# Ten of block one's gate tiles made by seven products behind the input norm, with 22 left as filler in the mixers

## The chip, the cores and the metric

The kernel runs on one core of one Trainium2 chip. What is measured is the time of one launch in microseconds (us), the median of three runs. A profiled execution stands beside them; its trace gives start and length of every instruction.

## The reference, cut to what matters

Two transformer blocks over 1024 tokens of width 1024, in fp32. Block one is a layer norm, one wide product, four mixers of width 256 (RET, RWKV, GLA, HGRN), and a gated merge of them:

```
x = layer_norm(x, ln_in_w, ln_in_b)
z = x @ w_in                                 # 1024 x 7696
z_ret, z_rwkv, z_gla, z_hgrn, z_gate = split_cols(z, ...)
branches = (retnet(z_ret), rwkv7(z_rwkv), gla(z_gla), hgrn2(z_hgrn))
for n in range(4):
    merged += sigmoid(z_gate[:, n*1024:(n+1)*1024]) * (branches[n] @ w_branch[n])
```

Behind it come a mixing product, a second norm, a feed-forward part and block two, which the change leaves alone. The change is about z_gate: 4096 columns, 32 tiles of 128.

## The kernel before, in words

**Products.** x lies on the chip transposed (features on partitions) as two parts, x_hi and x_lo, and each fp32 product is made as three: hi by hi, lo by hi, hi by lo. A *strip* is 128 columns of a weight matrix: eight blocks of 128 rows, three products, two halves of 512 tokens, so 48 matmuls of 128x512. Its weights come by a DMA on SP into w_raw, ACT copies them to w_hi (L2084), POOL makes w_lo = w_raw - w_hi (L2103). Two places hold such strips, so that weights run two half-strips or strips ahead of TensorE (class Stream, from L1949). L2152 is the matmul of a plain strip.

**The stages.** `phases` (L5806) calls in turn: `first_group` (0 to 121 us), the RWKV mixer (to 496), HGRN (to 681), GLA (to 871), RET (to some 990), `middle_group` and `second_group`. `first_group` (L3691) makes the input norm (class FirstNorm, L3477: L3680 is its last DVE step) and 16 half strips, (h, j) for h in 0..1 and j in 0..7, the columns of RWKV. ACT mixes each with its neighbour token (L3752), DVE adds the shifted part (L3744, L3746). POOL splits the strips in a loop at the end of the function; each engine's program is one list, done in order.

**The filler.** The mixers' own steps are short matmuls with chains of DVE, ACT and POOL between them. So that TensorE isn't idle there, class Filler (L209) gives it *runs* of six matmuls of 128x512 (L291) of other work: the z columns that the next mixer needs, transposes of its values (a *turn*, two runs a tile, at L284, some 0.6 us a run), and the 32 gate tiles, which go to DRAM and are read back by `middle_group`. A strip is eight runs. Ahead of each step of a mixer class Ring lays as many runs as a table says:

```
def start(self, pe, name, unit):
    self.fill.chunks(pe, self.table.get((name, unit), 0), self.place[name, unit])
    back = self.place[name, unit] - self.pairs
    if back >= 0:
        pe.wait_ge(self.sig["out_" + self.steps[back][0]], self.steps[back][1] + 1)
```

The tables stand by hand in `phases`, a number for each step's name: each mixer has four units n = 0 to 3. Runs left over go at the mixer's end (`rest`, L301). A half strip that is done is copied by ACT from PSUM (L335), which then makes the next w_hi; POOL makes its w_lo before the next thing in its own list (L339 to L347). So where the runs end decides which work of ACT and POOL stands ahead of a mixer's own.

**The steps that the text speaks of.** RWKV: `norm` (ACT L1390, TensorE L1250), `tr1` (DVE L1509, TensorE L1256), X8, TW32, TW64, TA and U (small products with a wait each), `c0` (DVE L1589, TensorE L1328). HGRN and GLA: levels `l0` to `l7` (POOL L1031, L1033 and L1037, TensorE L658), `kt` (TensorE L671, transposes of keys), `psi` (L676, the product for the state; DVE L967 then makes the new state), `y` (L685). RET: `score` (L662), `kt`, `psi`, `y`, `var`, `mean`; its copy before psi is DVE L949.

**The seven products.** In `middle_group` pairs of gate tiles of block two are made by Winograd's form of Strassen's scheme: the product of 256 columns by 1024 tokens is cut in two by two by two, and seven products of 4 row blocks x 3 = 12 matmuls (84 in all) do what 96 do by strips. It needs four sums of x (the forms t1 to t4, class GateForms, L3273: DVE L3293 and L3300, ACT L3315 for their hi part), four sums of weight blocks per pair, and adds of the results. Class GateSevens (L3327) does products (L3404) and adds; class Feed (L2551) brings weights as *units* of 128x512 in six slots and five places: ACT L2659 makes hi, POOL L2686 makes lo, L2663 makes sums of weights.

## Time and profile before

| what | us |
| --- | --- |
| median of three runs | 3285.53 (3285.08 to 3286.27) |
| the profiled execution | 3288.68 |
| its span | 3286.5 |
| TensorE busy | 3244.4 (99%) |
| DVE / ACT / POOL busy | 1872.9 / 1347.6 / 1352.3 |

The span is the time from the first to the last instruction in the trace; some 2.2 us lie around it. TensorE's mean granted clock was 0.997 of its full speed. A row of a timeline reads: start, length, engine, line, operation, result <- operands, sizes, count, and in brackets how long the engine was idle before it and what released it.

### The profile page before, as it was taken

What the parts mean: (1) busy time and instruction counts of PE and PEld (TensorE: products, weight loads), DVE (VectorE), ACT (ScalarE), POOL (GpSimd) and SP (SyncE); (2) the same over time, 40 slices, a digit from 0 to 9 for tenths busy, and PEclk for the clock granted to TensorE, in tenths of its full rate; (3) what the DMA queues carried; (4) which work ended last, traced back from release to release, by engine and by line L of the source; (5) the groups of instructions that cost most, each with busy time, mean ns of one, the idle gap of its engine ahead of it and who ended that gap; (6) DMA issues with size and microseconds to landing.
All of it is one profiled execution on the core that took longest, in us unless ns stands there. A gap on an engine that the chain in (4) does not pass through costs nothing.

```text
span 3286.5 us, 48647 instructions
## 1 busy us (share of the span) xinstructions
PE 3244.4 (99%) x19042; PEld 2622.2 (80%) x19042; DVE 1872.9 (57%) x2504; ACT 1347.6 (41%) x2153; POOL 1352.3 (41%) x850
## 2 busy tenths in 40 slices
PE   9999999999999999999999999999999999999998
PEld 7877787777778878888788878888886888888886
DVE  6333425646446779777783446434663266555678
ACT  5333324343224464333443355224423353445444
POOL 4312124545322846544525654541112665454102
PEclk9999999999999999999999999999999999999999
DMA  4221213232537323333563344332343332345664
GB/s 129 75 65 59 69 56 114 79 100 72 147 93 247 114 80 101 97 106 100 200 200 100 94 120 123 103 117 87 114 133 108 121 96 80 120 157 196 217 194 148
DMA packets 413346, 388.83 MB, mean 118 GB/s; under 512 B 23584, under 2 KB 329632, under 8 KB 410304
## 3 DMA queue, kind: packets, MB, share of 16 engines
q1 hardware_dynamic: 386208, 341.68, 33.8%
q10 hardware_dynamic: 26912, 44.05, 3.9%
q8 instruction: 153, 2.51, 0.3%
q14 instruction: 73, 0.60, 0.1%
HBM read 295.58 MB, written 90.08 MB: 117 GB/s over the span
## 4 chain that ended last, share of the span: by engine, by line
PE 45%; DVE 3%; ACT 1%; issue 1%; POOL 0%; DMA 0%; DVEq 0%; ACTq 0%
PE psum L2152 18%; PE psum L5169 9%; PE psum L2792 8%; PE psum L3404 5%; PE psum L1737 2%; PE psum L1780 1%; PE psum L2828 1%; DVE ffn_form_lo L5158 0%; PE psum L1767 0%; DVE conv L3167 0%; DVE acc L5205 0%; ACT w_hi L2084 0%; PE psum L1755 0%; PE psum L1757 0%; DVE w_lo L2686 0%
## 5 line engine op out<-in xcount | busy, mean ns | idle before, releaser
L2103 POOL TENSOR_TENSOR w_lo<-w_raw,w_hi 128x1024 fp32r<-128x1024 f32 (+1 forms) x226 | 548.1, 2425 | 964.0 <-ACT w_hi L2084 962.0
L2084 ACT ACTIVATE w_hi<-w_raw 128x1024 fp32r<-128x1024 f32 (+1 forms) x227 | 234.6, 1034 | 396.2 <-PE psum L2152 338.9
L291 PE MATMUL psum<-x_hi,w_hi 128*128 128x512 f32 x832 | 355.0, 427 | 3.1 <-ACT gate L335 3.0
L291 PE MATMUL psum<-x_hi,w_lo 128*128 128x512 f32 x832 | 326.9, 393 | 0.0
L291 PE MATMUL psum<-x_lo,w_hi 128*128 128x512 f32 x832 | 326.4, 392 | 0.0
L2152 PE MATMUL psum<-x_hi,w_hi 128*128 128x512 f32 x816 | 312.6, 396 | 3.7 <-DVE w_lo L2112 1.9
L2152 PE MATMUL psum<-x_lo,w_hi 128*128 128x512 f32 x816 | 308.0, 390 | 0.0
L2152 PE MATMUL psum<-x_hi,w_lo 128*128 128x512 f32 x816 | 307.9, 390 | 0.0
L2686 POOL TENSOR_TENSOR w_lo<-w_raw,w_hi 128x512 fp32r<-128x512 f32 x117 | 159.0, 1360 | 127.5 <-ACT w_hi L2659 117.3
L291 PEld LDWEIGHTS psum<-x_hi,w_hi 128*128 128x128 f32 x832 | 156.8, 188 | 48.8 <-issue 14.9
L2152 PEld LDWEIGHTS psum<-x_hi,w_hi 128*128 128x128 f32 x816 | 153.2, 188 | 39.9 <-issue 5.1
L291 PEld LDWEIGHTS psum<-x_hi,w_lo 128*128 128x128 f32 x832 | 156.7, 188 | 35.0
L291 PEld LDWEIGHTS psum<-x_lo,w_hi 128*128 128x128 f32 x832 | 157.2, 189 | 31.9 <-issue 5.8
L2152 PEld LDWEIGHTS psum<-x_lo,w_hi 128*128 128x128 f32 x816 | 153.5, 188 | 33.7 <-issue 2.2
L2152 PEld LDWEIGHTS psum<-x_hi,w_lo 128*128 128x128 f32 x816 | 153.6, 188 | 32.1
L335 ACT ACTIVATE gate<-psum 128x512 f32<-128x512 f32 x115 | 68.1, 592 | 222.3 <-PE psum L291 216.2
L2792 PE MATMUL psum<-x_hi,w_lo 128*128 128x512 f32 x368 | 143.2, 389 | 0.0
L2792 PE MATMUL psum<-x_lo,w_hi 128*128 128x512 f32 x368 | 143.2, 389 | 0.0
L2792 PE MATMUL psum<-x_hi,w_hi 128*128 128x512 f32 x368 | 143.2, 389 | 0.0
L2659 ACT ACTIVATE w_hi<-w_raw 128x512 fp32r<-128x512 f32 x144 | 88.9, 627 | 104.1 <-PE psum L5169 31.3
L5169 PE MATMUL psum<-mlp_form_hi,w_hi 128*128 128x512 f32 x288 | 112.1, 389 | 0.1
L5169 PE MATMUL psum<-mlp_form_hi,w_lo 128*128 128x512 f32 x288 | 112.0, 389 | 0.0
(849 smaller groups left out, 7997.2 us busy)
## 6 DMA issues: line engine op xcount, KB each, us to landing
w_raw<-in_w_in SPq DMA_DIRECT2D x99, 512.0 KB, 4.5
merge_raw<-gates ACTq DMA_DIRECT2D x48, 512.0 KB, 4.7
x_raw<-mlp_forms SPq DMA_DIRECT2D x76, 256.0 KB, 3.4
gates<-gate SPq DMA_DIRECT2D x32, 512.0 KB, 3.0
w_raw<-in_w_mlp_out SPq DMA_DIRECT2D x54, 256.0 KB, 3.3
mlp_forms<-mlp_staged SPq DMA_DIRECT2D x13, 1024.0 KB, 3.9
w_raw<-in_w_ffn_up SPq DMA_DIRECT2D x24, 512.0 KB, 3.9
ffn_x_raw<-ffn_forms SPq DMA_DIRECT2D x46, 256.0 KB, 3.7
```

Source lines behind the costliest of these rows:

```text
L291: last = pe.matmul(bank, w[:, k, :], x[:, k, half(h)], start=(k == 0 and j == 0), stop=(k == KT - 1 and j == 2))
L335: act.activation(self.c.gate[:, n % 2, half(h)], self.c.ps[:, 6 + h, :], ACT.Copy).then_inc(self.sig["g_taken"], 1)
L1737: last = pe.matmul(c.ps[:, 7, :], w[:, k, :], x[:, k, half(h)], start=(k == 0 and j == 0), stop=(k == 7 and j == 2))
L1780: last = pe.matmul(self.o_bank(n)[:, i, :], self.pt[:, n % 2, 2 * i + b, :], self.vs[g][:, j - 1 + b, 64 * h:64 * h + 64], start=(b == hav ...
L2084: act.activation(self.view(self.c.wh, i), self.view(self.c.wr, i), ACT.Copy).then_inc(self.sig["w_hi"], 1)
L2103: pool.tensor_tensor(self.view(self.c.wl, i), self.view(self.c.wr, i), self.view(self.c.wh, i).bitcast(F32), ALU.subtract).then_inc(self.s ...
L2152: last = pe.matmul(self.bank(t, h)[0:m, :], w[:, k, col:col + m], x(k)[:, 512 * h:512 * h + 512], start=(k == 0 and n == 0), stop=(k == nk ...
L2659: act.activation(self.places[self.place_of(u)][0], self.raw(u), ACT.Copy).then_inc(self.sig["f_hi"], 1)
L2686: pool.tensor_tensor(lo, self.raw(u), hi.bitcast(F32), ALU.subtract).then_inc(self.sig["f_pool"], 1)
L2792: last = pe.matmul(self.in_bank(p, n), w[:, k, :], v(k), start=(k == 0 and i == 0), stop=(k == KT // 2 - 1 and i == 2))
L3404: last = pe.matmul(self.bank(p, n), w[:, k, :], v(k), start=(k == 0 and i == 0), stop=(k == KT // 2 - 1 and i == 2))
L5169: ins = pe.matmul(self.bank(i, m), w[:, 0, P * m:P * m + P], x, start=(first and n == 0), stop=(last and n == 2))
```

## The change

Gate tiles 22 to 31 leave the mixers. `first_group` makes them as five pairs by GateSevens, after its 15th half strip and before the 16th. The forms come from a new class FirstForms: DVE first puts x together from its two parts (six quarters of that are POOL's), then makes four sums; ACT copies four hi parts, DVE makes three lo parts and POOL one. The first unit's split with its sums, `feed.lo(pool, 0)`, stands in POOL's loop at half strip 8, units 1 and 2 at 13, units 3 and 4 ahead of the last one. Semaphores are used again under new names. The mixers' gate tiles go from 12, 5, 6 and 9 to 8, 4, 4 and 6, and the tables lose 80 runs: 32 in RWKV, 9 in HGRN, 15 in GLA, 24 in RET. The last argument of each mixer (12 for 15, and so on) says where SP waits for stores.

```diff
     def at(self, name, n):
-        return self.core.counted.get(name, 0) + n
+        return self.here.get(name, self.core.counted.get(name, 0)) + n
+
+    def renew(self, name, old, count):
+
+        self.made[name], self.here[name] = self[old], count
...
@@ -2716,11 +2720,11 @@
 class Freed:
 
 
-    def __init__(self, st, sig, n, done=None):
-        self.st, self.sig, self.n, self.tile = st, sig, n, done
+    def __init__(self, st, sig, n, done=None, own=2):
+        self.st, self.sig, self.n, self.tile, self.own = st, sig, n, done, own
 
     def slot(self, sp, r):
-        if r >= 2:
+        if r >= self.own:
...
+class FirstForms:
...
+    MADE, SPLIT = ("t1", "t3", "t2", "t4"), ("t2", "t3", "t4")
+    READ = {"t1": 4, "t3": 3, "t2": 5, "t4": 5}
...
+    def whole(self, eng, h, k, end):
+        eng.wait_ge(self.sig["x_lo"], KT * h + end)
+        return eng.tensor_tensor(self.x_in[:, k:end, half(h)], self.c.xh[:, k:end, half(h)].bitcast(F32),
+                                 self.c.xl[:, k:end, half(h)].bitcast(F32), ALU.add)
+
+    def whole_pool(self, pool, h, k):
+        self.whole(pool, h, k, k + 2).then_inc(self.sig["x_whole"], 1)
...
+    def sum(self, dve, i):
+
+        x11, x12, x22, x21 = (self.raw[n] for n in self.MADE)
+        if i == 0:
+            self.whole(dve, 1, KT // 2, KT).then_inc(self.sig["gate_t"], 1)
+            return
+        out, x, y = ((x11, x12, x11), (x12, x22, x12), (x22, x22, x11), (x21, x21, x22))[i - 1]
+        dve.wait_ge(self.sig["x_whole"], self.sig.at("x_whole", 6))
+        dve.wait_ge(self.sig["gate_t"], self.sig.at("gate_t", i))
+        dve.tensor_tensor(out, x, y, ALU.subtract).then_inc(self.sig["gate_t"], 1)
+
+    def hi(self, act, name):
+        act.wait_ge(self.sig["gate_t"], self.sig.at("gate_t", self.MADE.index(name) + 2))
+        act.activation(self.his[name], self.raw[name], ACT.Copy).then_inc(self.sig["gate_t_hi"], 1)
...
+    def lo(self, dve, name):
+        self.low(dve, name, 0, 4).then_inc(self.sig["gate_t_lo"], 1)
+
+    def lo_pool(self, pool, k):
+        self.low(pool, "t1", k, k + 2).then_inc(self.sig["gate_t1_lo"], 1)
...
-            self.st.freed_held(pe, self.number(p, n) // 2, hold=1)
+            self.st.freed_held(pe, self.number(p, n) // 2, hold=self.hold)
...
+        def gates_by_sevens(n):
+            flat_place = lambda buf, i: [flat(buf[:, st.place(i)])[:, 512 * b:512 * b + 512] for b in range(2)]
+            slots = [*(more_raw[:, i, :] for i in range(4)), *flat_place(core.wr, n - 1)]
+            places = [(more_w[:, 0, :], more_w[:, 1, :]), *zip(flat_place(core.wh, n - 2), flat_place(core.wl, n - 2)),
+                      *zip(flat_place(core.wh, n - 1), flat_place(core.wl, n - 1))]
+            feed = Feed(sig, slots, places, w_sums, Freed(st, sig, n, own=4))
+            forms = FirstForms(core, sig, raw, low, t_his)
+            def quarter(k0, h):
+                return (lambda k: core.xh[:, k0 + k, half(h)]), (lambda k: core.xl[:, k0 + k, half(h)])
+            x = {"b11": quarter(0, 0), "b21": quarter(4, 0), "b22": quarter(4, 1), **{t: forms.x(t) for t in FirstForms.MADE}}
+            sevens = GateSevens(core, st, sig, feed, forms, x, sum(p is not None for p in st.places), 0)
+            for i in range(gate_tiles[0], gate_tiles[1], 2):
+                sevens.plan(a["w_in"], GATE0 + i * P, gates, (i - KT) * P)
+            feed.elsewhere.update(range(1, sevens.count))
+            st.feeds.append(feed)
+            return feed, sevens, forms
...
+        HELD = 2 * KT - 1
+        for n, (h, j) in enumerate(strips):
+            if n == HELD:
+                st.hold()
+                feed, sevens, forms = gates_by_sevens(st.held)
...
+            st.load(sp, 6)
+            feed.fetch(sp, 3)
+            st.load_held(sp)
+            feed.fetch(sp, len(feed.loads) - 1)
             st.load(sp, len(st.strips))
...
+                if n == HELD:
+                    for p in range(sevens.count):
+                        sevens.tensor(pe, p)
+                if n >= HELD:
+                    sevens.left(pe, n - HELD)
...
-            mixes(2 * KT - 8)
+            mixes(2)
+            forms.hi(act, "t1")
+            feed.hi(act, 0)
+            mixes(1)
+            forms.hi(act, "t3")
+            forms.hi(act, "t2")
+            mixes(1)
+            forms.hi(act, "t4")
+            mixes(2)
+            for u in (1, 2):
+                feed.hi(act, u)
+            mixes(1)
+            for u in (3, 4):
+                feed.hi(act, u)
+            def resume(act, n):
+                if n in (4, 6):
+                    at = st.held + (n - 4) // 2
+                    st.hi(act, st.ends[at - 2], at + 1, True)
+            for p in range(sevens.count):
+                sevens.scalar(act, p, (lambda n: resume(act, n)) if p == sevens.count - 1 else None)
+            sevens.store(act, sevens.count - 1, "c12")
+            mixes(1)
+            sevens.all_stored(act)
...
-            shifts(2 * KT - 8)
+            forms.sum(dve, 0)
+            for i in range(1, 5):
+                forms.sum(dve, i)
+                shifts(1)
+            for name in FirstForms.SPLIT:
+                forms.lo(dve, name)
+                shifts(1)
+            for p in range(sevens.count):
+                sevens.vector(dve, p)
+            shifts(1)
...
+            for n, (h, j) in enumerate(strips):
+                if n == HELD:
+                    for u in (3, 4):
+                        feed.lo(pool, u)
+                    for p in range(sevens.count):
+                        sevens.gpsimd(pool, p)
+                    for i in range(2):
+                        at = st.held + i
+                        st.lo(pool, st.ends[at - 2], at + 1, True)
                 st.lo(pool, tiles[h, j][0])
+                if 2 <= n < 8:
+                    forms.whole_pool(pool, *((0, 0), (0, 2), (0, 4), (0, 6), (1, 0), (1, 2))[n - 2])
+                if n == KT:
+                    feed.lo(pool, 0)
+                if n in (KT + 3, KT + 4):
+                    forms.lo_pool(pool, 2 * (n - KT - 3))
+                if n == KT + 5:
+                    for u in (1, 2):
+                        feed.lo(pool, u)
...
-    slot = first_group(nc, core, a, k, z, col_strip(w, HGRN0, 0), col_strip(w, HGRN0 + 512, 0))
+    slot = first_group(nc, core, a, k, z, gates, (22, 32), col_strip(w, HGRN0, 0), col_strip(w, HGRN0 + 512, 0))
-        gate_tiles(fill, range(12))
+        gate_tiles(fill, range(6, 14))
-        gate_tiles(fill, range(12, 17))
+        gate_tiles(fill, range(14, 18))
-        gate_tiles(fill, range(17, 23))
+        gate_tiles(fill, range(18, 22))
-        gate_tiles(fill, range(23, 32))
+        gate_tiles(fill, range(6))
-                            dict(norm=3, tr1=8, tr2=1, J2=1, J4=1, J8t=1, X4=1, X8=2, TW16=1, Y16=1, TW32=2, Y32=1, TW64=2,
-                                 Y64=1, TA=2, TAt=1, PP=1, c0=2, c1=1, c2=1, c3=1, U=1, y=1, bg=1),
-                            for_hgrn, (col(GLA0 + 512),), (col(GLA0),), [(zt[:, n, :], rows(z_hgrn, n)) for n in (2, 0, 4)], 15)
+                            dict(norm=2, tr1=7, tr2=1, J2=1, J4=1, J8t=1, X4=1, X8=1, TW16=1, Y16=1, TW32=1, Y32=1, TW64=1,
+                                 Y64=1, TA=1, TAt=1, PP=1, c0=1, c1=1, c2=1, c3=1, y=1, bg=1),
+                            for_hgrn, (col(GLA0 + 512),), (col(GLA0),), [(zt[:, n, :], rows(z_hgrn, n)) for n in (2, 0, 4)], 12)
-                              lambda n: dict(var=1, l0=12 if n == 0 else 5, l1=1, l2=1, l3=1, l4=1, l5=1, l6=1, l7=1, kt=3,
-                                             psi=2, y=3 if n == 0 else 2) | (dict(l0=3, kt=4, psi=3) if n == 2 else {}),
+                              lambda n: dict(var=1, l0=10 if n == 0 else 4, l1=1, l2=1, l3=1, l4=1, l5=1, l6=1, l7=1, kt=2,
+                                             psi=2, y=3 if n == 0 else 2) | (dict(l0=3, kt=3) if n == 2 else {}),
-                               *between_rows(zt[:, 0:5:4, :], k["zero"])], 11)
+                               *between_rows(zt[:, 0:5:4, :], k["zero"])], 10)
-                              lambda n: dict(var=1, l0=9 if n == 0 else 5, l1=1, l2=1, l3=1, l4=1,
-                                             l5=1, l6=1, l7=1, kt=2 if n == 0 else 3, psi=2, y=3)
-                              | (dict(l0=3, kt=4, psi=3) if n == 1 else {}),
-                              for_ret, (col(GATE0 + 23 * P),), (col(GATE0 + 24 * P),),
+                              lambda n: dict(var=1, l0=7 if n == 0 else 3, l1=1, l2=1, l3=1, l4=1,
+                                             l5=1, l6=1, l7=1, kt=2, psi=2, y=2),
+                              for_ret, (col(GATE0),), (col(GATE0 + P),),
-                               *between_rows(zt[:, 1:6:4, :], k["zero"])], 11)
+                               *between_rows(zt[:, 1:6:4, :], k["zero"])], 9)
-                              lambda n: dict(score=3 if n == 0 else 2, kt=4, psi=2, y=2, var=3, mean=2), no_mixer,
-                              *((col_strip(a["w_branch"][1], c, 0, rows=2 * P, width=512), 2, P, 512) for c in (0, 512)), [], (0, 1, 3, 5, 9))
+                              lambda n: dict(score=2 if n == 0 else 1, kt=2, psi=1, y=2, var=2, mean=1), no_mixer,
+                              *((col_strip(a["w_branch"][1], c, 0, rows=2 * P, width=512), 2, P, 512) for c in (0, 512)), [], (0, 1, 2, 3, 6))

```

## Rows read from the trace of the kernel before

**Rows 1.** The page: busy time of each engine.

```profile
PE 3244.4 (99%) x19042; PEld 2622.2 (80%) x19042; DVE 1872.9 (57%) x2504; ACT 1347.6 (41%) x2153; POOL 1352.3 (41%) x850
```

**Rows 2.** Waits of TensorE, 125 to 1000 us: total, times, longest.

```profile
PE psum L658 <- POOLq L1037: 5.5, 14, 0.6
```

**Rows 3.** The chain that ended last, around 2060 to 2220 us: start, length.

```profile
2059.99 5.45 PE psum L2152 x24
...
2068.51 149.91 PE psum L3404 x660
```

**Rows 4.** Groups of instructions by line and form: busy time, mean ns of one.

```profile
L3315 ACT ACTIVATE gate_t_hi<-acc 128x2048 fp32r<-128x2048 f32 x4 | 7.6, 1905 | 0.0
...
L2659 ACT ACTIVATE w_hi<-w_raw 128x512 fp32r<-128x512 f32 x144 | 88.9, 627 | 104.1 <-PE psum L5169 31.3 <-DVE w_raw L5114 24.7 <-PE psum L3404 23.8
...
L2686 POOL TENSOR_TENSOR w_lo<-w_raw,w_hi 128x512 fp32r<-128x512 f32 x117 | 159.0, 1360 | 127.5 <-ACT w_hi L2659 117.3 <-DVE ffn_w_raw_more L2663 2.5 <-DVE w_raw L2663 2.5
```

**Rows 5.** Single lines' instructions: ns least, median, most; first and last start.

```profile
L2663 POOL TENSOR_TENSOR ffn_sum<-ffn_w_raw_more,w_raw x1: 1295/1295/1295, 1280.8 to 1280.8; 128x512 f32<-128x512 f32 x1
...
L3300 DVE TENSOR_TENSOR acc<-acc x4: 4307/4370/4376, 2028.7 to 2046.4; 128x2048 f32<-128x2048 f32 x4
```

**Rows 6.** Timeline of ACT and POOL, 86 to 92 us.

```profile
86.47 1.05 ACT L2084 ACTIVATE w_hi<-w_raw 128x1024 fp32r<-128x1024 f32 x1
91.32 0.69 ACT L3752 ACTIVATE rwkv_z<-psum,first_one_mu 128x512 f32<-128x512 f32 x1 [3.80 <-PE psum L2152]
...
87.59 2.39 POOL L2103 TENSOR_TENSOR w_lo<-w_raw,w_hi 128x1024 fp32r<-128x1024 f32 x1 [3.05 <-ACT w_hi L2084]
```

**Rows 7.** Windows: busy by engine (instructions), then granted clock, DMA share, GB/s.

```profile
24.00:27.00 3.00, 3.00 (x10) 2.19 (x9) 2.96 (x5) 1.37 (x2) 2.86 (x3) 0.62 0.06 16
27.00:30.00 3.00, 3.00 (x12) 2.46 (x11) 2.86 (x5) 1.09 (x2) 2.71 (x3) 0.81 0.00 0
```

**Rows 8.** Timeline of RWKV's steps c0, norm (second unit) and tr1.

```profile
197.75 0.69 DVE L1589 TENSOR_TENSOR rwkv_j2t<-rwkv_j2t,rwkv_m_t 128x512 f32<-128x512 f32 x1
198.94 0.38 PE L1328 MATMUL psum<-rwkv_state,rwkv_j2t 128*128 128x128 f32 x2
...
218.39 0.61 ACT L1390 ACTIVATE rwkv_l<-rwkv_jt 128x512 f32<-128x512 f32 x1
...
220.25 1.02 PE L1250 MATMUL psum<-rwkv_l,rwkv_heads 128*128 128x512 f32 x2
...
142.61 0.68 DVE L1509 TENSOR_TENSOR rwkv_j2t<-rwkv_j,rwkv_e_mid 128x512 f32<-128x512 f32 x1
...
143.84 0.60 PE L1256 MATMUL psum<-rwkv_ident,rwkv_j2t 128*128 128x128 f32 x4
```

**Rows 9.** Timeline of GLA: levels of TensorE, and POOL in the first unit.

```profile
785.17 0.68 PE L658 MATMUL psum<-gla_qe,gla_ke 64*64 64x64 f32 x16
...
798.90 0.69 PE L658 MATMUL psum<-gla_qe,gla_ke 64*64 64x64 f32 x32 [0.39 <-POOLq L1037]
...
706.70 2.38 POOL L2103 TENSOR_TENSOR w_lo<-w_raw,w_hi 128x1024 fp32r<-128x1024 f32 x1 [0.17 <-POOL gla_ke L1033]
```

**Rows 10.** Timeline of HGRN's first state update and of y behind it.

```profile
548.87 3.49 DVE L967 SCALAR_TENSOR_TENSOR hgrn_state<-hgrn_state,hgrn_end,hgrn_state_new 128x128 f32<-128x128 f32 x4
...
552.46 0.45 PE L685 MATMUL psum<-hgrn_qe,hgrn_state 128*64 128x128 f32 x4 [0.47 <-issue]
```

**Rows 11.** Timeline of RET's chain from score to psi.

```profile
938.51 1.16 PE L662 MATMUL psum<-mixer_z 64*128 64x128 f32 x16
...
945.94 0.68 DVE L949 COPY ret_k_tok<-psum 128x512 f32<-128x512 f32 x1
...
948.78 1.05 PE L676 MATMUL psum<-ret_v,ret_k_tok 128*128 128x128 f32 x8
```

**Rows 12.** Timeline of RET's first unit: score and the filler behind it.

```profile
882.14 1.16 PE L662 MATMUL psum<-mixer_z 64*128 64x128 f32 x16 [0.58 <-DVE mixer_z L866]
...
889.55 0.47 PE L291 MATMUL psum<-x_hi,w_hi 128*128 128x512 f32 x1 [1.94 <-ACT gate L335]
```

More of the change, by code:

```diff
@@ L123, in __init__ @@
         super().__init__()
-        self.core, self.phase, self.made = core, phase, {}
+        self.core, self.phase, self.made, self.here = core, phase, {}, {}
     def __getitem__(self, name):
@@ L3336, with __init__ @@
     OUT = ("c11", "c22", "c21", "c12")
-    def __init__(self, core, st, sig, feed, forms, x, place):
-        self.c, self.st, self.sig, self.feed, self.forms, self.x, self.place = core, st, sig, feed, forms, x, place
+    def __init__(self, core, st, sig, feed, forms, x, place, hold):
+        self.c, self.st, self.sig, self.feed, self.forms, self.x, self.place, self.hold = (
+            core, st, sig, feed, forms, x, place, hold)
         self.s1, self.u2, self.u3, self.c22 = (core.gate[:, i // 2, half(i % 2)] for i in range(4))
@@ L3699, in first_group @@
     eps, warm = mem("eps", [P, 1]), mem("warm", [P, 1])
+    more_w, more_raw = mem("w_more", [P, 2, T // 2], F32R), mem("w_raw_more", [P, 4, T // 2])
+    w_sums = [at_(f"first_w_sum{i}", [P, T // 2], F32, offset=OFF_TAIL + 2 * KB * i)[:, :] for i in range(2)]
+    low = at_("x_in_lo", [P, KT, T], F32R, offset=OFF_S)
+    t_his = {n: at_(f"first_{n}_hi", [P, KT // 2, T // 2], F32R, offset=OFF_S + (32 + 8 * i) * KB)[:, :, :]
+             for i, n in enumerate(FirstForms.MADE)}
     with ExitStack() as ctx:
@@ L3702, in first_group @@
         st = Stream(core, sig)
+        for i in range(6):
+            sig.renew(f"f_raw{i}", f"x1{i}", 16)
+        for i, name in enumerate(("gate_c11_stored", "gate_c12_stored", "gate_c21_stored", "gate_c22_stored",
+                                  "gate_t_hi", "gate_t_lo", "gate_t1_lo", "gate_s1")):
+            sig.renew(name, f"x0{i}", 16)
+        for name, old, count in (("gate_t", "off", KT), ("gate_sum", "x16", 16), ("f_hi", "x17", 16),
+                                 ("f_pool", "sq_added", KT - 1), ("f_mm", "sq", 2 * KT), ("x_whole", "pair_first", 1),
+                                 ("mixed", "sq_pair", 1), ("carry", "pair", 2), ("carried", "pair_late", 1),
+                                 ("centred", "sq_pair_late", 3), ("log", "shift", 1)):
+            sig.renew(name, old, count)
+        def gates_by_sevens(n):
[14 more added lines that the diff above has]
+            return feed, sevens, forms
         norm = FirstNorm(core, st, sig, raw, sq, total, ones[:, :], eps, w, b, rstd, warm)
@@ L3707, in first_group @@
         norm.plan_var(0)
-        for h, j in strips:
+        HELD = 2 * KT - 1
[3 more added lines that the diff above has]
+                feed, sevens, forms = gates_by_sevens(st.held)
             i = st.strip(col_strip(a["w_in"], RWKV0 + j * P, 0))
@@ L3771, in _ @@
             norm.tensor_sums(pe)
-            for h, j in strips:
+            for n, (h, j) in enumerate(strips):
                 t, i = tiles[h, j]
+                if n == HELD:
[3 more added lines that the diff above has]
+                    sevens.left(pe, n - HELD)
                 if (h, j) == (0, 0):
@@ L4028, in middle_group @@
         in_x = {"b11": quarter(0, 0), "b21": quarter(4, 0), "b22": quarter(4, 1), **{t: forms.x(t) for t in GateForms.MADE}}
-        sevens = GateSevens(core, st, sig, feed2, forms, in_x, sum(p is not None for p in st.places))
+        sevens = GateSevens(core, st, sig, feed2, forms, in_x, sum(p is not None for p in st.places), 1)
         for g in range(3):
```

26 lines of the change are left out of this document (20 added, 6 removed).

## The prediction, made before the changed kernel ran

> **What bounds the kernel now.** I read the busy times first: TensorE is busy 3244.4 of 3286.5 us [rows 1], and no other engine is above 57%. So the time is TensorE's work plus the few places where it waits; the change can only take work away or move waits. Next the waits of the mixer stretch, 125 to 1000 us: the longest entry is 5.5 us in 14 pieces, at L658, released by POOL [rows 2]. The mixers' steps wait little, because a run of filler (six matmuls) or more lies between any two of them. Last, the timeline around single steps: how long ahead of TensorE's step its releaser was done. That slack, held against the time of the run that is taken out in front of the step, is what decides here.
>
> **The work.** Ten strips of 48 matmuls leave the mixers (480, in 80 runs); five pairs of 84 come in (420). A half strip of 24 takes 5.45 us, 0.2271 each and 1.36 a run; the seven products' nearest row is 660 matmuls in 149.91 us, again 0.2271 each, without a wait inside [rows 3]. So -480 + 420 = -60, times 0.2271: **-13.6 us**. The units' transfers and stores go out by SP and ACT in that stretch; the cover is the same as in the row, DMA queues and copies beside 20 us of products a pair, so I cost them at nothing; a late unit would be a wait at L3404. Bounds: -13.6 (as there) to -9 (each pair's first unit late by one ACT copy of 0.63 [rows 4], and 1.5 us for the turn from strips to units).
>
> **The input norm.** ACT mixes strip 9 and makes w_hi of strip 11 until 86.47 + 1.05 = 87.52 us, POOL splits strip 11 from 87.59 on, in 2.39, and TensorE ends strip 10 at 91.3, where ACT's mix of it begins [rows 6]. The change puts on ACT, ahead of that mix, the copy of the form t1 (1.91) and the first unit's copy (0.63) [rows 4]: done at 90.05. On POOL comes, after the split of strip 10 and ahead of that of strip 11, this unit's split of 1.36 [rows 4] and three sums of 1.30 [rows 5], some 0.14 between them: 90.05 to 95.85. POOL's queue is in order, so the split of strip 11 ends at 98.25, and TensorE wants it at 91.3: **7.0** us. I take the order in the code over "it will be ready in time"; had the sums been made before, it would be 3.9 less. What a wait does to the clock: after TensorE's wait of 2 us at 21 to 23 us the granted clock was 0.62 over three us and 0.81 over three more [rows 7]; 3 x 0.38 + 3 x 0.19 = **1.7** us. Together 8.7; bounds 0 (slack in the split that I don't see) and 10.
>
> DVE's form sums are like those of L3300, 4.31 to 4.38 us each in all four places, though POOL's splits run in that stretch [rows 5]; a sum that stood behind a split would be longer. The Trainium skill ("SBUF — State Buffer", section "Who interferes with whom") states that a DVE instruction with two inputs in SBUF and a GpSimd instruction that reads SBUF lock each other out for the whole instruction; by that rule the first form sum would end about 1 us later, and the sum of this forecast would be 1 us higher. In this case the row decides, and it shows no such stretch.
>
> **RWKV, 32 runs fewer, 8 in each of four units.** At X8, TW32, TW64, TA and U the releaser is done over 2 us ahead: these cost nothing; what covers them is that slack and, but for U, the run that stays. Three steps have less slack than a run. c0: DVE's L1589 ends at 198.44, TensorE's L1328 starts at 198.94 [rows 8]: 0.50 against 1.36, so 0.86 lost, four times, 3.4. The norm's step: ACT's L1390 ends at 219.00, L1250 starts at 220.25 [rows 8]: 1.25, 0.1 lost, twice; at the first unit the slack is half of that, 0.8 lost; at the third both runs left are turns of the value tiles, half a run each, 1.8 lost: 2.8. tr1 of the first unit: L1509 ends at 143.29, L1256 starts at 143.84 [rows 8], 0.8 lost. **+7.0**; bounds 0 (DVE's chain starts from a TensorE step that comes earlier by as much) and 10.
>
> **HGRN and GLA, 24 fewer.** (a) Levels 1 to 6 take 785.17 to 798.90, 13.7 us, and end on a wait for POOL [rows 9]: they are paced at 2.3 us a level by POOL and DVE. The shorter l0 moves three to four turns into them, half a run each in place of a whole one, which a level can't give back: 2.7. (b) l0 of GLA's first unit, two runs less ahead of levels whose first products stand on POOL behind a split of 2.38 at 706.70 [rows 9]: all of it lost, 2.7. (c) HGRN's first kt: a strip now ends in the level before, and its split stands ahead of the step's own product on POOL: half a strip's split and copy, 1.6. (d) The state update: DVE's four L967 took 3.49, a POOL split of 2.39 beside them, and L685 waited 0.47 at 552.46 with three runs between [rows 10]. With two runs the same meeting costs 1.36 more, some 1.9. By the counts of runs, splits meet the update at GLA's first and HGRN's last unit (3.0 together) and two old meetings go (-0.9): 2.1. **+9.1**; bounds 2 (only b, in part) and 12.
>
> **RET, 24 fewer.** The chain behind a unit's scores: L662 at 938.51, DVE's masks, a reciprocal, two products, and the copy L949, ending 945.94 + 0.68 = 946.62; L676 follows at 948.78 [rows 11]. The steps are 10.27 apart, 8.1 of them the chain: 2.1 may go, while three runs leave (4.1). So 2.0 is lost at units 1 to 3: 6.0. The first unit's score already waited 0.58, so its run is a wait of 1.4 more; behind it the filler's bank waited 1.94 for ACT [rows 12], and with fewer runs the bank is asked for later, of which 1.2 goes. Its state update meets a split: 1.9. **+8.1**; bounds 2 and 10.
>
> **Sum.** -13.6 + 8.7 + 7.0 + 9.1 + 8.1 = **+19.3 us**. The profiled execution took 3288.68 us (its span 3286.5, and 2.2 around it), 3.15 above the median of 3285.53; its like would be 3308.0, and the median 3304.8. What a measurement can tell from no change is about 0.2%, 6.6 us.
>
> **Rivals.** *Faster* (0.17): ready times move ahead with TensorE. Each mixer chain starts from a TensorE step; if what I took for a fixed chain of DVE starts behind the very step that comes earlier, only its last piece counts, and if POOL's sums fall into its gaps no wait for strip 11 comes. Then -13.6 to -10, 3271.9 to 3275.5. For it: TensorE is busy 99% [rows 1], and the mixers' waits are few [rows 2], so they have been covered amply. Against it: slacks of 0.50 at c0 [rows 8] and 2.1 in RET [rows 11] are smaller than what goes. It decides where slacks exceed 1.36 a run taken out. *Same* (0.12): the mixers absorb it and only the wait for strip 11 comes: -13.6 + 8.7 = -4.9, 3280.6. *Slower still* (0.09), the change not doing what it says: the products of the first stretch stall where those of the middle don't, because strips, forms and units share POOL; one late split of 1.36 [rows 4] in each of five pairs on top of the forecast, 3311.6. It decides once POOL is over a unit behind at the first pair.
>
> **How the numbers follow.** Forecast 0.62, its own range 3292 to 3312: mixer terms at half and at their upper bounds. With the rivals: faster 0.17, same 0.13 (0.12 and a part of the forecast's low end), slower 0.70. The range, 3280 to 3313, takes in the case with the norm's wait alone; it leaves out the one in which all is hidden, and a little above.
>
> **What would show it.** In the changed kernel: 420 matmuls of L3404 in some 95.4 us, starting near 125; at 91 us a wait of TensorE at L2152 for POOL's w_lo, 7 us, and a granted clock under 0.9 in the 6 us behind it; new waits at L1328 (0.9, four), L1250 (0.1 to 1.8), L658 (5.5 to some 10), and L676 of RET (2.0, three). If strip 11 is split ahead of POOL's sums, the norm's term is wrong; if the stretch from the end of the first group to the middle one is shorter by 109 us and not by 85, the mixers' terms are.

## The result and the profile after

The changed kernel takes **3332.0 us** (median of four runs, 3331.8 to 3333.1) against 3285.9 for the kernel before in the same runs: 1.0138 times as long, 95% interval 1.0126 to 1.0151, so 46.1 us slower. The direction was forecast, the size (+19.3) was not, and the time lies above the range. One execution each of experiments 5 and 8 and of the kernel before took 4.6 to 9.0 ms, and the medians and ratios below leave it out, where experiment 8's expectation has it in (3322.4 for 3321.3).

Lines carry new numbers in the changed kernel: the products of the sevens L3404 are L3466, L2152 is L2156, L2103 L2107, L658 L662, L662 (RET's scores) L666, L671 L675, L676 L680, L685 L689, L1328 L1332, L1250 L1254, L1256 L1260, the filler L291 is L295; ACT's copy of a unit L2659 is now L2663, POOL's split of it L2690, its sums L2667, and DVE's form sums are L3363.

First the page after, busy time of each engine, against [rows 1]:

```profile
span 3331.1 us, 48775 instructions
...
PE 3247.0 (97%) x18982; PEld 2618.6 (79%) x18982; DVE 1942.7 (58%) x2563; ACT 1357.9 (41%) x2167; POOL 1412.7 (42%) x887
```

There are 60 matmuls fewer, and yet TensorE is 2.6 us *longer* busy: a matmul takes longer while the clock is low. Where the rest went is in TensorE's waits of the first 1050 us of the changed kernel (line, releaser: us in total, times, longest):

```profile
PE psum L662 <- POOLq L1041: 11.8, 17, 1.9
PE psum L2156 <- POOL w_lo L2107: 11.7, 2, 10.9
PE psum L680 <- DVE ret_k_tok L953: 7.0, 3, 2.4
PE psum L295 <- ACT gate L339: 3.9, 5, 1.4
PE psum L689 <- issue: 3.7, 2, 1.8
PE psum L1332 <- DVE rwkv_j2t L1593: 3.3, 4, 0.8
PE psum L666 <- DVE mixer_z L870: 2.7, 1, 2.7
PE psum L1254 <- ACT rwkv_l L1394: 2.7, 2, 2.0
```

The first is [rows 2] doubled. The second is new, one wait of 10.9 us in the first group. The third and the fifth to the eighth are the steps that the prediction named (psi of RET, y behind the state update, c0, RET's first score, the norm's step).

A table by stage, worked out from TensorE's instructions: a stage runs from its first step to the next one's, the last one to the end of the last matmul, "work" is the change in the number of 128x512 matmuls times 0.2271 us, "lost" is the change of the duration less the work. "Waits" sums idle times over 0.15 us, "clock" sums (1 - granted clock) x busy time over windows of 3 us; both are changes against before.

| stage | before | after | work | lost | waits | clock |
| --- | --- | --- | --- | --- | --- | --- |
| start to first RWKV step | 126.8 | 235.9 | +95.4 | 13.8 | 11.7 | 1.2 |
| to HGRN's first kt | 416.9 | 384.5 | -47.7 | 15.3 | 9.7 | 1.4 |
| to GLA's first kt | 182.4 | 181.2 | -9.5 | 8.3 | 7.4 | 2.4 |
| to RET's first kt | 164.9 | 148.6 | -23.2 | 6.8 | 4.7 | 3.4 |
| to the middle group | 106.4 | 89.5 | -28.6 | 11.7 | 6.8 | 4.5 |
| to the last matmul | 2278.5 | 2280.9 | 0 | 2.4 | 1.7 | 0 |

So 58.3 us lost against 13.6 saved, 44.6 in the spans (46.1 in the medians): some 42 us of it are waits, some 13 the clock, 3 neither column accounts for. Part of these 3 is how idle time is counted: a 128x512 matmul is recorded with 0.39 us though the next starts 0.23 behind it, and a wait counts as idle only from the recorded end. c0 shows it: its four waits are 0.82, and the step comes 0.97 to 0.99 us later than its work says. Over the 19 waits that the mixers have more than before, 0.16 each makes 3 us, by this estimate. The 2.4 of the last row come back in every kernel below (1.7 to 4.2); 1.7 of the 2.4 are waits that I have not followed.

**The long wait.** Timeline of ACT, DVE and POOL in the changed kernel around it (start, length, engine, line):

```profile
86.11 1.92 ACT L3367 ACTIVATE first_t_hi<-x_in 128x2048 fp32r<-128x2048 f32 x1 [0.47 <-DVE x_in L3363]
87.93 0.61 ACT L2663 ACTIVATE first_w_more<-first_w_raw_more 128x512 fp32r<-128x512 f32 x1
...
81.77 4.30 DVE L3363 TENSOR_TENSOR x_in<-x_in 128x2048 f32<-128x2048 f32 x1
...
86.73 2.28 DVE L3363 TENSOR_TENSOR x_in<-x_in 128x2048 f32<-128x2048 f32 x1
...
90.74 2.99 DVE L3363 TENSOR_TENSOR x_in<-x_in 128x2048 f32<-128x2048 f32 x1
...
95.45 2.90 DVE L3363 TENSOR_TENSOR x_in<-x_in 128x2048 f32<-128x2048 f32 x1
...
88.62 1.52 POOL L2690 TENSOR_TENSOR first_w_more<-first_w_raw_more,first_w_more 128x512 fp32r<-128x512 f32 x1 [4.69 <-ACT first_w_more L2663]
90.31 1.27 POOL L2667 TENSOR_TENSOR first_w_sum<-first_w_raw_more 128x512 f32<-128x512 f32 x1 [0.17 <-POOL first_w_more L2690]
91.66 3.20 POOL L2667 TENSOR_TENSOR first_w_sum<-first_w_sum,first_w_raw_more 128x512 f32<-128x512 f32 x1
94.94 1.27 POOL L2667 TENSOR_TENSOR first_w_raw_more<-first_w_raw_more 128x512 f32<-128x512 f32 x1
96.16 6.72 POOL L2107 TENSOR_TENSOR w_lo<-w_raw,w_hi 128x1024 fp32r<-128x1024 f32 x2
```

The queue is as forecast: POOL stands 4.69 us for ACT's copy of the unit with the split of strip 11 behind it, then makes the unit's split and three sums, then the two splits. But one sum takes 3.20 instead of 1.27, and the first of the two splits took 4.4 instead of 2.4 (6.72 for both); each began within 1 us behind a DVE form sum. (Both ends of the wait lie some 1.5 us earlier than in the prediction: TensorE asks at 89.8, ACT's copy of the unit is done at 88.5.)

**The clock.** Windows of the changed kernel (busy of PE, PEld, DVE, ACT, POOL with instructions, then the granted clock, DMA share, GB/s):

```profile
90.00:100.00 10.00, 0.00 (x0) 0.00 (x0) 8.36 (x6) 5.14 (x4) 9.68 (x5) 0.62 0.00 0
100.00:103.00 3.00, 2.30 (x6) 1.85 (x7) 0.00 (x0) 0.00 (x0) 2.88 (x2) 0.50 0.37 99
103.00:106.00 3.00, 3.00 (x9) 2.32 (x8) 0.00 (x0) 0.00 (x0) 0.00 (x0) 0.50 0.90 252
...
974.00:977.00 3.00, 3.00 (x12) 2.65 (x12) 1.34 (x4) 0.00 (x0) 0.70 (x1) 0.58 0.57 176
```

TensorE comes back at 100.7 and works at half speed, 1.2 of 2.4 GHz, for about 5 us. The last row is RET, behind a wait of 2.4 us. The clock's share is the least steady number of this table. Experiments 1, 2 and 5 have the same mixers, with psi waits of 2.39, 2.32 and 2.32 us in each, and their clock column over the four mixer rows sums to 7.4, 7.6 and 9.9, for 11.7 here. In experiment 1 the first two of these waits have no dip behind them; the first, in its timeline and its window:

```profile
967.05 1.13 PE L680 MATMUL psum<-ret_v,ret_k_tok 128*128 128x128 f32 x8 [2.39 <-DVE ret_k_tok L953]
967.00:970.00 3.00, 2.95 (x17) 2.64 (x18) 1.61 (x5) 0.45 (x1) 1.26 (x1) 1.00 0.81 223
```

There RET's stage takes 86.7 us for 89.5. Three single waits of the mixers, in the timeline of the changed kernel:

```profile
302.86 0.46 PE L1332 MATMUL psum<-rwkv_state,rwkv_j2t 128*128 128x128 f32 x2 [0.82 <-DVE rwkv_j2t L1593]
...
744.89 0.45 PE L689 MATMUL psum<-hgrn_qe,hgrn_state 128*64 128x128 f32 x4 [1.83 <-issue]
...
973.43 2.05 PE L680 MATMUL psum<-ret_v,ret_k_tok 128*128 128x128 f32 x8 [2.39 <-DVE ret_k_tok L953]
```

c0 waits 0.82 (forecast 0.86), the met state update 1.83 (1.9), RET's psi 2.39, then 2.32 and 2.31 (2.0).

### The profile page after: what moved, and what is told of

Its sections match the earlier page's. It is cut to its first block and busy times, and to the rows that moved or that the text cites. A ratio compares the mean times of both kernels' runs of the same rounds, so it can differ in the third digit from the quotient of the medians.

```text
span 3331.1 us, 48775 instructions
## 1 busy us (share of the span) xinstructions
PE 3247.0 (97%) x18982; PEld 2618.6 (79%) x18982; DVE 1942.7 (58%) x2563; ACT 1357.9 (41%) x2167; POOL 1412.7 (42%) x887
## 3 DMA queue, kind: packets, MB, share of 16 engines
q1 hardware_dynamic: 384928, 336.44, 32.9%
## 5 line engine op out<-in xcount | busy, mean ns | idle before, releaser
L2107 POOL TENSOR_TENSOR w_lo<-w_raw,w_hi 128x1024 fp32r<-128x1024 f32 (+1 forms) x216 | 533.6, 2471 | 899.4 <-ACT w_hi L2088 897.9
L2088 ACT ACTIVATE w_hi<-w_raw 128x1024 fp32r<-128x1024 f32 (+1 forms) x217 | 224.1, 1033 | 405.7 <-PE psum L2156 338.3
L2156 PE MATMUL psum<-x_hi,w_hi 128*128 128x512 f32 x816 | 313.6, 397 | 15.5 <-POOL w_lo L2107 11.7
L2156 PE MATMUL psum<-x_hi,w_lo 128*128 128x512 f32 x816 | 308.4, 391 | 0.0
L2156 PE MATMUL psum<-x_lo,w_hi 128*128 128x512 f32 x816 | 308.3, 391 | 0.0
L295 PE MATMUL psum<-x_hi,w_hi 128*128 128x512 f32 x672 | 295.7, 440 | 3.9 <-ACT gate L339 3.9
L295 PE MATMUL psum<-x_hi,w_lo 128*128 128x512 f32 x672 | 267.3, 398 | 0.0
L295 PE MATMUL psum<-x_lo,w_hi 128*128 128x512 f32 x672 | 266.9, 397 | 0.0
L2690 POOL TENSOR_TENSOR w_lo<-w_raw,w_hi 128x512 fp32r<-128x512 f32 x122 | 165.6, 1358 | 133.7 <-ACT w_hi L2663 121.9
L2156 PEld LDWEIGHTS psum<-x_hi,w_hi 128*128 128x128 f32 x816 | 153.5, 189 | 53.6 <-issue 18.7
L2156 PEld LDWEIGHTS psum<-x_lo,w_hi 128*128 128x128 f32 x816 | 153.9, 189 | 33.6 <-issue 2.2
L2156 PEld LDWEIGHTS psum<-x_hi,w_lo 128*128 128x128 f32 x816 | 153.7, 188 | 32.4
L295 PEld LDWEIGHTS psum<-x_hi,w_hi 128*128 128x128 f32 x672 | 128.8, 192 | 43.2 <-issue 15.0
L295 PEld LDWEIGHTS psum<-x_hi,w_lo 128*128 128x128 f32 x672 | 128.4, 191 | 29.4
L295 PEld LDWEIGHTS psum<-x_lo,w_hi 128*128 128x128 f32 x672 | 129.1, 192 | 26.5 <-issue 6.0
L3508 DVE TENSOR_TENSOR gate<-psum,gate 128x512 f32<-128x512 f32 x91 | 61.7, 690 | 151.0 <-PE psum L3466 146.1
L2796 PE MATMUL psum<-x_hi,w_hi 128*128 128x512 f32 x368 | 143.2, 389 | 0.0
L2796 PE MATMUL psum<-x_lo,w_hi 128*128 128x512 f32 x368 | 143.2, 389 | 0.0
L2796 PE MATMUL psum<-x_hi,w_lo 128*128 128x512 f32 x368 | 143.2, 389 | 0.0
L2663 ACT ACTIVATE w_hi<-w_raw 128x512 fp32r<-128x512 f32 x149 | 92.1, 627 | 112.0 <-PE psum L5325 31.3
L339 ACT ACTIVATE gate<-psum 128x512 f32<-128x512 f32 x95 | 55.9, 591 | 175.1 <-PE psum L295 169.8
```

Source lines behind the costliest of these rows:

```text
L295: last = pe.matmul(bank, w[:, k, :], x[:, k, half(h)], start=(k == 0 and j == 0), stop=(k == KT - 1 and j == 2))
L339: act.activation(self.c.gate[:, n % 2, half(h)], self.c.ps[:, 6 + h, :], ACT.Copy).then_inc(self.sig["g_taken"], 1)
L2088: act.activation(self.view(self.c.wh, i), self.view(self.c.wr, i), ACT.Copy).then_inc(self.sig["w_hi"], 1)
L2107: pool.tensor_tensor(self.view(self.c.wl, i), self.view(self.c.wr, i), self.view(self.c.wh, i).bitcast(F32), ALU.subtract).then_inc(self.s ...
L2156: last = pe.matmul(self.bank(t, h)[0:m, :], w[:, k, col:col + m], x(k)[:, 512 * h:512 * h + 512], start=(k == 0 and n == 0), stop=(k == nk ...
L2663: act.activation(self.places[self.place_of(u)][0], self.raw(u), ACT.Copy).then_inc(self.sig["f_hi"], 1)
```

## The experiments

Each kernel below is the changed one with the edit shown, run in rounds with the kernel before, whose median was 3286.1 to 3286.7 in them. The ratios are known to about 0.15%, 5 us. A difference of 2 to 6 us from the changed kernel's 3332.0 is therefore read from the waits and the stages of the trace, with the time beside it.

**1. The unit's work on POOL in two pieces.**

```diff
                 if n == KT:
-                    feed.lo(pool, 0)
+                    feed.lo_alone(pool, 0)      # the split
+                    feed.sum_alone(pool, 0, 0)
+                if n == KT + 1:
+                    feed.sum_alone(pool, 0, 1)
+                    feed.sum_alone(pool, 0, 2)
```

> The changed kernel (3332.0 us) with the first unit's work on POOL cut up: its split and one sum at half strip 8, the other two sums behind the split at half strip 9. Theory: the wait of 10.9 us for strip 11 is POOL's queue, whose idle time between two splits is 3.05 us, so pieces of 2.9 and 2.6 us fit and the block of 7.5 us doesn't. Expected: that wait under 1.5 us, the clock dip behind it (some 2.7 us) gone too, 3318 to 3321 us. Rival: ACT's copies of t1 and of the unit are what is late; then POOL starts as late as before, the wait stays over 7 us, and the time at 3328 to 3332.

Measured 3326.4 us (ratio 1.0124, 1.0107 to 1.0141). Neither theory's number: the wait became 6.3, and the time lies between the two. POOL's timeline shows why:

```profile
88.89 1.52 POOL L2697 TENSOR_TENSOR first_w_more<-first_w_raw_more,first_w_more 128x512 fp32r<-128x512 f32 x1 [4.70 <-ACT first_w_more L2663]
90.58 1.27 POOL L2667 TENSOR_TENSOR first_w_sum<-first_w_raw_more 128x512 f32<-128x512 f32 x1 [0.17 <-POOL first_w_more L2697]
91.81 4.40 POOL L2107 TENSOR_TENSOR w_lo<-w_raw,w_hi 128x1024 fp32r<-128x1024 f32 x1
```

POOL is idle for 4.70 us, and for the last 3.0 of them the split behind could run (its w_hi was made by 85.9). Taking two sums out of the front gave back 4.6 of the 10.9 us; most of the rest is that what still stands in front waits for ACT. And the split again takes 4.40 beside a DVE form sum.

**2. DVE's form sums out of the way.** POOL as in the changed kernel:

```diff
             forms.sum(dve, 0)
-            for i in range(1, 5):
-                forms.sum(dve, i)
-                shifts(1)
+            forms.sum(dve, 1)
+            shifts(1)
+            forms.sum(dve, 2)
+            shifts(3)
+            forms.sum(dve, 3)
+            shifts(1)
+            forms.sum(dve, 4)
```

(the low parts and ACT's copies of t2 and t4 follow at later half strips.)

> The changed kernel with DVE's third and fourth form sum moved behind later half strips, so that none of them runs beside POOL's three weight sums and the split of strip 11; POOL's own order is left. Theory of the locked port: these two stretched a POOL sum from 1.27 to 3.20 us and the split from 2.4 to 4.3, 3.8 of the 10.9 us; the wait falls to 7.0 and the time to 3327 or 3328. Rival (DVE doesn't touch POOL here, the long POOL instructions have another cause): wait 10.9 and 3332.

Measured 3329.6 us (1.0130, 1.0115 to 1.0145). The wait and POOL's timeline:

```profile
PE psum L2156 <- POOL w_lo L2107: 7.7, 2, 6.9
```

```profile
92.03 1.27 POOL L2667 TENSOR_TENSOR first_w_sum<-first_w_sum,first_w_raw_more 128x512 f32<-128x512 f32 x1
93.37 1.26 POOL L2667 TENSOR_TENSOR first_w_raw_more<-first_w_raw_more 128x512 f32<-128x512 f32 x1
94.59 4.65 POOL L2107 TENSOR_TENSOR w_lo<-w_raw,w_hi 128x1024 fp32r<-128x1024 f32 x2
```

With nothing changed on POOL the sum takes 1.27 again and the two splits 4.65 for 6.72: 10.9 became 6.9, the 7.0 of the prediction. What was missing there is DVE. The stage lost 11.3 us instead of 13.8. The time is 2.4 less, above the 3327 to 3328 expected and within the intervals of both, so it is the rows that show this, not the time.

**3. The first group alone.** The old tables and gate tiles of `phases` (the removed lines of the diff) beside the new first group; ten tiles are made twice.

> The old tables and all 32 gate tiles in the mixers, beside the five pairs in the first group: ten tiles are made twice. It prices the first group alone: 420 matmuls at 0.2271 are 95.4 us, its waits and clock 13.7 in the trace, so 3285.5 + 109.1 = 3394.6 us. The mixers then wait as before the change (some 14 us in all). Rival: the mixers' waits come from what the first group leaves behind (semaphores, slots, the clock); then they wait 40 us here too, and the time is over 3410.

Measured 3397.2 us (1.0337, 1.0321 to 1.0352), 110.5 over the kernel before: 95.4 of work and 15.1 lost. Each mixer's stage takes what it took before within 2 us (RET 106.4 and 106.4), and the level products wait as in [rows 2]:

```profile
PE psum L662 <- POOLq L1041: 5.7, 14, 0.6
```

So the first group leaves nothing behind that makes the mixers wait, and its loss doesn't depend on their tables. The rest, 46.1 - 110.5 = -64.4 us, is the mixers' part, where the work alone would be -109.0: they lose 44.6.

**4. RET's run moved from var to psi.**

```diff
-                              lambda n: dict(score=2 if n == 0 else 1, kt=2, psi=1, y=2, var=2, mean=1), no_mixer,
+                              lambda n: dict(score=2 if n == 0 else 1, kt=2, psi=1 if n == 0 else 2, y=2,
+                                             var=2 if n == 0 else 1, mean=1), no_mixer,
```

> The changed kernel with one run of filler in RET moved, in units 1 to 3, from the step var to the step psi. Theory: psi waits 2.3 us three times for DVE's chain behind the scores, and the clock falls behind each wait (1.5 us each time), while the stretch from y over var to mean has room. Expected: the three waits go to about 0.95 each, 1.36 gained each and most of the clock's part: 3324 to 3328 us. Rival: var's stretch has no room, and what psi gains var loses: 3332.

Measured 3329.0 us (1.0128, 1.0113 to 1.0143), 3 less, where 4 to 8 were expected. Timeline and windows of RET:

```profile
974.45 1.13 PE L680 MATMUL psum<-ret_v,ret_k_tok 128*128 128x128 f32 x8 [1.01 <-DVE ret_k_tok L953]
...
1006.19 1.10 PE L627 MATMUL psum<-ret_tail,ret_head_mean 128*128 128x512 f32 x2 [1.55 <-ACT ret_tail L710]
```

```profile
974.00:977.00 3.00, 2.55 (x15) 2.31 (x16) 1.55 (x5) 0.85 (x2) 1.26 (x1) 1.00 1.01 265
```

The psi waits fall to 1.0 and 0.9 as worked out, and behind them the clock stays at 1.00, where it was 0.58 behind 2.4 (and 1.00 behind the same 2.4 in experiment 1, so part of that gain is chance). In one unit of three, var's stretch had no room: a new wait of 1.55 behind an ACT step. From RET's first kt on the stage is 6.0 us shorter, but the span only 3.3: the first group, GLA and the last stage are 1.5, 1.8 and 1.8 us longer and the first two mixers' stages 1.8 and 0.6 shorter, none of which the edit touches. In GLA it is the clock.

**5. The unit's work behind the split of strip 11.** The pieces of experiment 1 one half strip later, and DVE as in experiment 2:

```diff
-                if n == KT:
-                    feed.lo(pool, 0)
+                if n == KT + 1:
+                    feed.lo_alone(pool, 0)
+                    feed.sum_alone(pool, 0, 0)
+                if n == KT + 2:
+                    feed.sum_alone(pool, 0, 1)
+                    feed.sum_alone(pool, 0, 2)
```

> The changed kernel (3332.0 us) with both parts of the wait for strip 11 treated: all of the first unit's work on POOL stands behind the split of strip 11, in two pieces (2.9 and 2.6 us) at half strips 9 and 10, and DVE's third and fourth form sum come later, as in the run before. Theory: cutting up alone left a wait of 6.3 because POOL stood waiting for ACT's copy of the unit with the split of strip 11 behind it; with the split ahead nothing is left of the 10.9 but what a sum of DVE stretches, under 1 us. Expected 3318 to 3321 us, the first RWKV step at 223 to 224 us instead of 235.9. Rival: strip 12 or 13 waits instead, as POOL has 3.05 us free a half strip and gets 2.9, 2.6, 2.4 and 2.4 in a row: waits of 2 to 3 us, 3322 to 3325.

Measured 3321.3 us (1.0105, 1.0087 to 1.0124). The first RWKV step comes at 226.4 for 235.9, where the theory said 223 to 224. The waits of TensorE from 80 to 130 us:

```profile
PE psum L2156 <- POOL w_lo L2107: 1.8, 2, 1.3
PE psum L3486 <- POOL w_lo L2690: 0.8, 1, 0.8
```

and POOL ahead of the longer of them:

```profile
100.18 4.42 POOL L2107 TENSOR_TENSOR w_lo<-w_raw,w_hi 128x1024 fp32r<-128x1024 f32 x1
```

So 9.5 of the 13.8 us are back, 8.3 of them in the waits. A clock dip at 24 us, worth some 1.7 us, that the changed kernel's profile has and this one doesn't, behind the same wait of 2.05 us, is not the edit's doing. What is left are form sums that meet splits, in part the rival's case. What most of the first group's loss hangs on is thereby shown: the order on POOL, and DVE's sums.

**6. Runs moved inside the mixers.**

```diff
-                            dict(norm=2, tr1=7, ..., c0=1, ...)
+                            dict(norm=2, tr1=6, ..., c0=2, ...)
-                              ... (dict(l0=3, kt=3) if n == 2 else {}),      # HGRN
+                              ... (dict(l0=5, kt=3) if n == 2 else {}),
-                              lambda n: dict(var=1, l0=7 if n == 0 else 3, ...   # GLA
+                              lambda n: dict(var=1, l0=7 if n == 0 else 5 if n == 2 else 3, ...
```

> The changed kernel with runs moved inside mixers, to be read stage by stage. RWKV: one run from tr1 to c0. The slack theory: the four waits of 0.82 at c0 go, the first unit's tr1 waits 1.36 longer, the others' slack at tr1 (2.9) covers it: RWKV 1.9 us shorter. HGRN and GLA, third unit: l0 gets two runs more (3 to 5), taken from what is left at the mixer's end. Theory: the turns of the value tiles then fall into l0 and not into the levels, which wait 3.8 and 3.3 us there with a clock dip behind; each mixer 3 to 5 us shorter. Rival: the levels are paced by POOL whatever stands in front; then the two runs are simply waiting less at the end, and the stage keeps its length. In all 3323 to 3327 against 3332 of the rival.

Measured 3325.8 us (1.0117, 1.0101 to 1.0133), 6.2 less, in the expected range. Waits of the mixers:

```profile
PE psum L662 <- POOLq L1041: 9.3, 16, 1.9
PE psum L689 <- issue: 7.4, 5, 1.8
...
PE psum L1254 <- ACT rwkv_l L1394: 2.7, 2, 2.0
...
PE psum L1260 <- DVE rwkv_j2t L1513: 2.5, 1, 2.5
```

The line of L1332 is gone, and L1260 waits 2.5 for 1.1, as worked out: the stage to HGRN's kt lost 11.3 instead of 15.3. That is 4.0 for the expected 1.9, but the kernels here with the changed kernel's table in RWKV lost 13.4 to 15.3 in this stage, the clock being the difference, and two waits at L1220 (1.5 us together) are gone too, for a reason that I have not followed. The levels wait 2.5 us less, but L689 5 times instead of twice: the ends of the strips have moved, and other units' splits now meet the state update. The new wait of 1.83 at 877 us has a split at 875.3 beside DVE's update at 875.5. HGRN's stage gained 3.2, GLA's 2.2, where 3 to 5 each were expected. Of the rival it shows this much: what is won at the levels is in part paid at y.

**7. Three pairs instead of five.** First group as in experiment 5 with `(26, 32)` for `(22, 32)`; 9, 5, 5 and 7 gate tiles in the mixers; the tables:

```diff
+   RWKV  dict(norm=3, tr1=7, ..., X8=1, TW32=1, TW64=1, TA=1, c0=2, ...)      # no U
+   HGRN  as before the change
+   GLA   l0=(9, 3, 5, 4)[n], kt=(2, 3, 3, 2)[n], psi=2, y=3 if n == 0 else 2
+   RET   score=3 if n == 0 else 1, kt=3, psi=2, y=2, var=2, mean=1
```

> A version meant to beat both: three pairs instead of five in the first group (with the order of e5), 26 gate tiles left in the mixers, and the 48 runs taken only from steps where the trace of the changed kernel shows that taking them cost nothing: in RWKV X8, TW32, TW64, TA, U and tr1, in GLA some of psi, y, l0 and kt, in RET score, kt, var and mean of the later units. c0, the norm's step, HGRN's table and RET's psi stay. Theory: the work falls by 36 matmuls, 8.2 us; the first group adds 1 us, the first unit's tr1 0.8 and RET's first score 0.5: 3285.9 - 8.2 + 2.3 = 3280 us. Rival: moved ends of strips put splits in front of other steps, 5 to 10 us of new waits and clock dips: 3283 to 3290.

Measured 3286.6 us (median of ten) against 3286.4: ratio 1.0001, 0.9991 to 1.0011. It doesn't beat the kernel before by the expected 6 us; it equals it, which is the rival's case. Its waits up to 1040 us:

```profile
PE psum L662 <- POOLq L1041: 6.4, 15, 0.8
PE psum L295 <- ACT gate L339: 5.8, 5, 2.0
PE psum L689 <- issue: 2.5, 3, 1.2
```

c0, the norm's step and RET's psi have left the list. By the stages of the profiled execution, in the table's order, it loses 2.5, 0.7, 1.4, -2.3, 5.9 and 2.6 us: 10.8 against 8.2 saved (the profiled execution was the longest of the ten, 3291.0). RWKV gave up 24 runs for 0.7 us (24 of its 32 were free), RET 15 for 5.9.

**8. Five pairs with all that helped**: the edits of 4 and 5, and of 6 those of RWKV and HGRN.

> All that helped, put together with five pairs and the reduced tables otherwise kept: the order of e5 on POOL and DVE, RET's run moved from var to psi, RWKV's from tr1 to c0, two runs more in l0 of HGRN's third unit. If the parts add up: 3322.4 (e5) - 3.0 (e4) - some 4.5 (of e6's 6.2) = 3315 us. Theory: the rest, 29 us over the kernel before, is what 80 runs fewer cost whatever their order, since the steps' chains on DVE, ACT and POOL don't get shorter; the waits in the mixers still sum to 30 us or more. Rival: the loss was a matter of where runs stood; then it comes under 3300.

Measured 3308.5 us (three executions, 3308.3, 3308.5 and 3314.0; ratio 1.0075, 1.0055 to 1.0095). The parts add up, with 5 us more. Its waits (30 to 1040 us):

```profile
PE psum L662 <- POOLq L1041: 10.2, 16, 1.9
PE psum L689 <- issue: 5.2, 3, 1.8
PE psum L680 <- DVE ret_k_tok L953: 2.9, 3, 1.0
PE psum L1254 <- ACT rwkv_l L1394: 2.7, 2, 2.0
```

So 22 to 24 of the 46.1 us were order, by the ratio and by the medians, and the rest is still there. The mixers wait 35 us, as the theory had it, and the time stays over the rival's 3300. By the stages it loses 2.2, 11.7, 5.1, 5.4, 7.3 and 1.8 us. Whether another table does better stays open; the moves tried inside the mixers brought new waits elsewhere.

## Why the prediction was right in direction and wrong in size

- **What bounds, and the work.** TensorE at 99% bounded, and -13.6 us held: in experiment 3 the first group's 420 matmuls cost 110.5, and 95.4 + the waits and clock seen there (18.5 against 6.5 us of waits, 5.3 against 3.2 of clock) is 109.5. The mixers' 480 were never run by themselves, and their part of the work is the count.
- **The input norm, +8.7, measured 13.8.** The mechanism, the place and the 7.0 of the queue were right (experiment 2 shows 6.9). The step that failed is the reading of [rows 5]: "DVE's form sums are like those of L3300, 4.31 to 4.38 us each in all four places, though POOL's splits run in that stretch". I took four equal durations for an undisturbed one. They are four disturbed ones: the same sum takes 2.28 us at 86.73, where POOL is idle. Four times the sum had stood behind a split, as the kernel before shows for the first and the last of them:

```profile
2028.53 2.42 POOL L2103 TENSOR_TENSOR w_lo<-w_raw,w_hi 128x1024 fp32r<-128x1024 f32 x1 [1.98 <-ACT w_hi L2084]
2028.74 4.37 DVE L3300 TENSOR_TENSOR acc<-acc 128x2048 f32<-128x2048 f32 x1
2044.85 3.74 POOL L2103 TENSOR_TENSOR w_lo<-w_raw,w_hi 128x1024 fp32r<-128x1024 f32 x1 [2.88 <-ACT w_hi L2084]
2046.36 4.38 DVE L3300 TENSOR_TENSOR acc<-acc 128x2048 f32<-128x2048 f32 x1
```

And the hold-up goes both ways: where DVE starts first it is POOL's instruction that grows, the split from 2.4 to 4.4 and the sum from 1.27 to 3.20, and this was the 3.9 us that were missing. (The same rows had it: the split at 2044.85 takes 3.74 behind a DVE instruction that started at 2044.05.) The Trainium skill's rule ("SBUF — State Buffer", section "Who interferes with whom"), that a DVE instruction with two inputs in SBUF and a GpSimd instruction that reads it lock each other out for the whole instruction, agrees with every row here, down to a DVE instruction of one column: L3843, 128x1 from two SBUF operands, takes 0.14 us at 86.00 and 1.23 at 88.93, until POOL's split that started at 88.62 ends at 90.14. I had set the rule aside on the row's word. Its effect is larger than the 1 us that I had worked out from it, for I had let it act on DVE alone.
- **RWKV and HGRN's first kt, +7.0 and 1.6, measured 15.3.** c0 (3.3 for 3.4), the norm's step (2.7 for 2.8), tr1 of the first unit (1.1 for 0.8) and HGRN's first kt (1.25 for 1.6; the wait ends at the cut, and the table books it in the next row) are the size forecast. Missing are the levels of HGRN's first unit (2.3 us of waits for 0.4 before, where l0 went from 12 to 10, a term that I had for GLA's first unit but not for HGRN's), clock (1.4), and some 3.5 us of small waits and of time that shows no idle time over 0.15 us; the 0.16 us a wait from the result's section is part of it.
- **HGRN and GLA up to RET's kt, +7.7 by the same cuts, measured 15.1.** The state updates came as written: 1.90 and 0.99 more at the two units named, and 0.5 each back at the two old meetings. The turns in the levels are the failed term, 2.7 for both mixers: at the third units alone the stretch up to kt lost 5.3 and 4.6 us, waits and, behind them, clock. RET's first score, which with the bank behind it was to cost 0.2, cost 1.5.
- **RET, +7.9 from its first kt on, measured 11.7.** psi is 2.39, 2.32, 2.31 for 2.0 three times; the state update of the first unit met no split (0 for 1.9). In this profile the stretch behind each psi wait took 1.4 to 1.7 us longer, a clock dip that the sum did not have.
- **The clock.** I priced it once, at the 7 us wait, and nowhere in the mixers. [rows 7] showed a dip behind a wait of 2 us, and three of my own terms were waits of 2 us. Over the mixers it came to 11.7 us in this profile and to 7.4, 7.6 and 9.9 in the others with the same mixers. This is the second failed term, put at nothing without a reason, and the larger one. But no single row gives its price: the wait of [rows 7] stands at the same place, with 2.05 or 2.06 us, in every kernel here, and in the profiles of experiments 4, 5 and 6 the clock behind it stays at 1.00.
- **The rivals.** The faster one, that ready times move ahead with TensorE, is out: the slack read from the trace predicted the waits at c0, the norm's step, tr1, HGRN's first kt and psi within 0.4 us each. That the products stall in the first stretch is out as well: no wait over 0.8 us at them in any kernel here.

In short: forecast losses 32.9 us, measured 58.3. Of the 25 that were missing 3.9 are DVE and POOL in each other's way, 7 to 12 the clock in the mixers, the rest levels and what the stages' columns leave open. That the direction came out right is not luck: with the terms as measured the losses are over four times what the work saves.

## What to carry to other kernels

Filler of known length between the steps of a chain can be priced before it is taken out: read the time from the releaser's end to the step, and what exceeds it is lost; then add to waits of 2 us what the clock may take behind them, as a range from nothing to the dip that rows of the same kernel show, for the same wait has it in one execution and not in the next. Equal durations are no proof of undisturbed ones: compare an instruction with its own kind at a place where the other engine is idle. And an in-order queue is blocked by the first piece that waits for someone as much as by the work that stands in it: put new work behind what TensorE needs next, not in front.
